# Context products of the first layer's experts: 512 columns wide, even and odd inner steps on separate groups of the array

## The reference, cut to what matters

```
def ec_moe(h, w_r, w1, w3, w2):
    cap = max(1, EC_CAPACITY * n // N_EXPERTS)            # 64 for x, 32 for context
    gate, idx = lax.top_k(jnp.swapaxes(aff, 1, 2), cap)   # each of 16 experts takes cap tokens
    xin = jax.vmap(lambda hb, ib: hb[ib])(h, idx)
    hid = silu(einsum('becd,edf->becf', xin, w1)) * einsum('becd,edf->becf', xin, w3)
    ye = einsum('becf,efd->becd', hid, w2) * gate[..., None]
    # the rows of ye are added back at their tokens' places
```

## Time and profile before

| | |
|---|---|
| median of 3 runs | 4251.18 us (4249.46 to 4256.13) |
| the profiled execution, its own time | 4257.33 us |
| its span, first to last instruction | 4255.5 us |
| mean granted TensorE clock | 0.979 of full speed |
| PE busy | 4008.4 us, 94% of the span |
| expert stage of the first layer | from 2447.6 to about 3002.5 us of the span |

### The profile page before, as it was taken

One profiled execution on the slowest core, in us unless ns is written; L12 is line 12 of the kernel. 1 busy time (PEld: TensorE's weight loads), 2 busy tenths in 40 slices (PEclk: granted clock), 3 DMA queues, 4 the chain that ended last, 5 costly groups with the idle time before them and its releaser, 6 DMA issues. The chain is left out here.

```text
span 4255.5 us, 65552 instructions
## 1 busy us (share of the span) xinstructions
PE 4008.4 (94%) x28448; PEld 2718.6 (64%) x28448; DVE 1677.8 (39%) x2603; ACT 1050.9 (25%) x2204; POOL 816.8 (19%) x640
## 2 busy tenths in 40 slices
PE   8999999999999899898999799999899999979888
PEld 6788889887888667566555443333576678833332
DVE  3685755374444442627434300000436364421102
ACT  2212522222111221616211321112315152221111
POOL 2100023113451021112233101000121234400000
PEclk9999999999999999999999899999999999989999
DMA  3584300122232212010112399999320102389997
GB/s 111 207 280 146 90 16 4 54 90 74 85 101 75 67 56 87 6 60 1 60 60 99 129 379 388 388 386 356 105 87 26 60 21 99 119 327 428 426 427 307
DMA packets 194194, 668.89 MB, mean 157 GB/s; under 512 B 11750, under 2 KB 75942, under 8 KB 169334
## 3 DMA queue, kind: packets, MB, share of 16 engines
q1 hardware_dynamic: 188022, 644.01, 40.1%
q0 software_dynamic: 5888, 20.70, 1.6%
HBM read 642.52 MB, written 22.15 MB: 156 GB/s over the span
## 5 line engine op out<-in xcount | busy, mean ns | idle before, releaser
L521 PE MATMUL psum<-arena 128*128 128x264 f32 (+2 forms) x7280 | 1829.8, 414 | 46.1 <-ACT arena L1513 19.4
L521 PEld LDWEIGHTS psum<-arena 128*128 128x128 f32 x7280 | 1386.7, 191 | 485.6 <-issue 47.9
L1397 PE MATMUL psum<-arena 128*64 128x512 f32 x3072 | 697.7, 601 | 43.7 <-DMA arena<-in_w_e 39.4
L1397 PEld LDWEIGHTS psum<-arena 128*64 128x64 f32 x3072 | 211.7, 137 | 466.8 <-issue 425.4
L553 ACT ACTIVATE arena<-psum 128x256 f32<-128x256 f32 (+2 forms) x405 | 169.3, 418 | 910.0 <-PE psum L521 878.8
L452 POOL TENSOR_TENSOR arena<-arena 128x512 f32<-128x512 f32 (+1 forms) x114 | 162.1, 1422 | 1025.6 <-PE psum L521 1025.6
L2367 DVE TENSOR_TENSOR arena<-arena,psum 128x512 f32<-128x512 f32 x32 | 22.0, 687 | 787.2 <-PE psum L1405 532.5
L382 PE MATMUL psum<-arena 128*128 128x265 f32 (+2 forms) x1120 | 257.8, 388 | 3.3 <-ACT arena L3059 3.3
L382 PEld LDWEIGHTS psum<-arena 128*128 128x128 f32 (+1 forms) x1120 | 209.8, 189 | 43.5 <-ACT arena L3059 3.7
L2813 PE MATMUL psum<-arena 64*64 64x64 f32 x7424 | 226.1, 219 | 8.7 <-issue 4.5
L2813 PEld LDWEIGHTS psum<-arena 64*64 64x64 f32 x7424 | 224.2, 135 | 11.7 <-issue 8.9
(11 more groups left out here) (417 smaller groups left out, 3916.4 us busy)
## 6 DMA issues: line engine op xcount, KB each, us to landing
arena<-in_w_e SPq DMA_DIRECT2D x192, 2048.0 KB, 12.8
arena<-in_w_in SPq DMA_DIRECT2D x38, 2048.0 KB, 8.1
arena<-in_w_ada SPq DMA_DIRECT2D x24, 2048.0 KB, 8.4
arena<-in_ffn_up SPq DMA_DIRECT2D x22, 1024.0 KB, 7.5
arena<-in_w_branch SPq DMA_DIRECT2D x6, 2048.0 KB, 8.2
arena<-in_ffn_down SPq DMA_DIRECT2D x8, 1408.0 KB, 8.1
arena<-in_w_in SPq DMA_DIRECT2D x16, 512.0 KB, 4.4
arena<-in_w_out SPq DMA_DIRECT2D x4, 2048.0 KB, 8.1
```

The costliest lines, as they stand in the source:

```text
L521: mm = pe.matmul(PS[:, bank, 0:cn], loaded, moved, start=fresh and k == 0, stop=k == h - 1, skip_group_check=not fresh)
L1397: mm = pe.matmul(PS[c * HD:c * HD + HD, b + (m > 0), :], x(kk), w[:, k, c * BW:c * BW + BW], start=(kk == 0), stop=(kk == KT - 1))
```

## The change

The context block has, per inner step, two matmuls of 512 columns in place of four of 256. Even inner steps go to the column groups 0 and 1 of the array, odd ones to the groups 2 and 3. So the partitions 0 to 63 of bank b+2 collect the sum over the even steps, with 512 columns on each of two groups of 32 partitions, and the partitions 64 to 127 the sum over the odd steps; the bank is full, and gate, up and down use it one after the other. The two sums are added at eviction: ACT copies the upper half to on-chip memory (`part_c`, semaphore c_part), DVE adds it to the lower half (`sum_c`, semaphore c_sum).

With it:

- PE waits for the sum of gate(e) before the context block of up(e), first half.
- The hidden context rows lie on 64 partitions with 512 columns. Their four transposes have 64 rows x 128 columns as stationary operand and stream 64 columns, where they had 128 rows x 64 columns and streamed 128; the copy after them (L1793 now) is one instruction instead of two.
- ACT: silu_c(e+1) stands ahead of take_ye(e), and reads on-chip memory; take_ye's context part is a copy, a wait for the sum and two pieces of 32 x 512 instead of four of 32 x 256.
- DVE: three sums per expert are added; sum_c("down", 15) stands ahead of `spread` and `add_tokens` after the last expert. `layer_scalars` moves ahead of the first sum.

```
+        HIDC, CPART = [H, H + BW], {"gate": H + 2 * BW, "up": H + 3 * BW, "down": H + 2912}
+        c_order = [("gate", 0), ("up", 0)]
+        for e in range(N_EXP):
+            c_order += [("gate", e + 1), ("down", e), ("up", e + 1)] if e + 1 < N_EXP else [("down", e)]
+        c_step = {x: i + 1 for i, x in enumerate(c_order)}
+        low, high = (0, HD), (HD, P)
...
+                    if half == 0 and m == 1:
+                        wt(pe, "c_sum", c_step["gate", e])
                     for k in range(4):
                         kk = half * 4 + k
-                        for c in range(4):
-                            mm = pe.matmul(PS[c * 32:c * 32 + 32, b + 2, (m > 0) * CTX:(m > 0) * CTX + CTX], xc(kk),
-                                           w[:, k, c * CTX:c * CTX + CTX], start=(kk == 0), stop=(kk == KT - 1))
+                        for c in range(2):
+                            r = (k % 2 * 2 + c) * 32
+                            mm = pe.matmul(PS[r:r + 32, b + 2, :], xc(kk), w[:, k, c * BW:c * BW + BW],
+                                           start=(kk < 2), stop=(kk >= KT - 2))
...
-                        tr = pe.transpose(PS[0:HD, b + 2, c * P:c * P + P], A[:, hid + BW + c:hid + BW + CTX:4], ident)
+                        hidc = HIDC[e % 2] + c
+                        tr = pe.transpose(PS[:, b + 2, c * HD:c * HD + HD], A[0:HD, hidc:hidc + BW - c:4], ident[0:HD, 0:HD])
...
+            def part_c(kind, e):
+
+                if kind == "up" and e:
+                    wt(act, "c_sum", c_step[kind, e - 1])
+                wt(act, "slab_used", slab_at[e, ("gate", "up", "down").index(kind), 1] + 1)
+                inc(nc.scalar.activation(at(CPART[kind], BW, *low), PS[HD:P, 3 * (e % 2) + 2, :], ACT.Copy), "c_part")
...
+                    part_c("gate", e)
+                    wt(act, "c_sum", c_step["gate", e])
+                    hidden = at(HIDC[e % 2], BW, *low)
+                    inc(nc.scalar.activation(hidden, hidden, ACT.Silu), "siluc")
...
-                    for c in range(4):
-                        r = slice(c * 32, c * 32 + 32)
-                        ins = nc.scalar.activation(at(yec + c * CTX, CTX, q * 32, q * 32 + 32),
-                                                   PS[r, b + 2, CTX:2 * CTX], ACT.Copy,
+                    part_c("down", e)
+                    wt(act, "c_sum", c_step["down", e])
+                    for c in range(2):
+                        ins = nc.scalar.activation(at(yec + c * BW, BW, q * 32, q * 32 + 32),
+                                                   at(CPART["down"], BW, c * 32, c * 32 + 32), ACT.Copy,
...
                 if e + 1 < N_EXP:
                     silu_x(e + 1)
+                    silu_c(e + 1)
                 take_ye(e)
-                if e + 1 < N_EXP:
-                    silu_c(e + 1)
+                if e + 1 < N_EXP and not last:
+                    part_c("up", e + 1)
...
+            def sum_c(kind, e):
+                wt(dve, "c_part", c_step[kind, e])
+                part = at(CPART[kind], BW, *low)
+                inc(V.tensor_tensor(at(HIDC[e % 2], BW, *low) if kind == "gate" else part, part,
+                                    PS[0:HD, 3 * (e % 2) + 2, :], ALU.add), "c_sum")
...
                 if not last:
+                    sum_c("up", e)
                     wt(dve, "siluc", e + 1)
-                    ins = V.tensor_tensor(at(hid + BW, CTX), at(hid + BW, CTX), PS[:, b + 2, CTX:2 * CTX], ALU.mult)
+                    wt(dve, "c_sum", c_step["up", e])
+                    hidc = at(HIDC[e % 2], BW, *low)
+                    ins = V.tensor_tensor(hidc, hidc, at(CPART["up"], BW, *low), ALU.mult)
...
+                if not last:
+                    if e + 1 < N_EXP:
+                        sum_c("gate", e + 1)
+                    sum_c("down", e)
                 if e + 1 < N_EXP:
                     hidden(e + 1)
```

More of the change, by code:

```diff
@@ L1391, in expert_slab, with half_product @@
                 return at(ES[j % n_slots], SLOT).rearrange("p (k n) -> p k n", k=4)
-            def half_product(b, w, half, x, xc, m, groups=0):
+            def half_product(b, w, half, x, xc, m, e, groups=0):
                 for k in range(4):
@@ L1417, in up @@
                 half_product(3 * (e % 2), w, half, lambda kk: at(XS[e // 2 % 2] + kk * P + e % 2 * CAP, CAP),
-                             lambda kk: at(XSC[e // 4 % 2] + kk * P + e % 4 * CAPC, CAPC), m,
+                             lambda kk: at(XSC[e // 4 % 2] + kk * P + e % 4 * CAPC, CAPC), m, e,
                              groups=e // 4 + 1 if half == 0 and m == 0 else 0)
@@ L1436, in down @@
                 half_product(3 * (e % 2), w, half, lambda kk: at(turned + kk * CAP, CAP),
-                             lambda kk: at(turned + BW + kk * CAPC, CAPC), 2)
+                             lambda kk: at(turned + BW + kk * CAPC, CAPC), 2, e)
             wt(pe, "cols", 1)
@@ L1761, in silu_x @@
                 inc(nc.scalar.activation(at(HID[e % 2], BW), PS[:, 3 * (e % 2), :], ACT.Silu), "silu")
+            def part_c(kind, e):
[3 more added lines that the diff above has]
+                inc(nc.scalar.activation(at(CPART[kind], BW, *low), PS[HD:P, 3 * (e % 2) + 2, :], ACT.Copy), "c_part")
             def silu_c(e):
                 if not last:
-                    wt(act, "slab_used", slab_at[e, 1, 1] + 1)
-                    inc(nc.scalar.activation(at(HID[e % 2] + BW, CTX), PS[:, 3 * (e % 2) + 2, 0:CTX], ACT.Silu), "siluc")
+                    part_c("gate", e)
+                    wt(act, "c_sum", c_step["gate", e])
+                    hidden = at(HIDC[e % 2], BW, *low)
+                    inc(nc.scalar.activation(hidden, hidden, ACT.Silu), "siluc")
             def take_hidden(e):
@@ L1773, in take_hidden @@
                 if not last:
[L1774 to L1777, removed]
+                    ins = nc.scalar.activation(at(turned + BW, CTX).rearrange("p (h c s) -> p c h s", h=2, s=CAPC),
+                                               PS[:, b + 2, 0:CTX].rearrange("p (c h s) -> p c h s", c=4, h=2), ACT.Copy)
                 inc(ins, "hid_taken")
@@ L1809, in _ @@
             silu_c(0)
+            if not last:
+                part_c("up", 0)
             for e in range(N_EXP):
@@ L2396, in _ @@
                 spread(PTG[0], 0, "spread_x", SEQ)
-            hidden(0)
             if not last:
                 layer_scalars(step, l + 1)
+                sum_c("gate", 0)
+            hidden(0)
             for e in range(N_EXP):
```

## The result

The changed kernel takes 4265.26 us (median of 7 runs, 4261.99 to 4269.58) against 4251.31 for the kernel before (7 runs): a ratio of 1.0032, with an interval of 1.0023 to 1.0042. It is 14 us slower.

What follows compares the result with a forecast made beforehand. PE's blocks were taken to bound the expert stage; ACT and DVE count only where PE waits. -0.9 + 5.5 + 0.8 + 3.0 + 0.4 = +8.8 us on the 4251.18 median gave 4260.0 us, range 4252 to 4266.

Steps and rivals of the forecast that it cites:

- The step that split the block into rounds: Context block, 96 times: columns set the time, excess sits at the ends; 1.855 against 1.865 us, -0.9 us in all.
- Rivals 1 and 2: Context blocks: records cost, per round (4253 us; 0.20 together with rival 3) or per record on the issue path (4230; 0.03).
- Rival 5: Context blocks: groups with different weights do not run side by side; block 3.6 us instead of 1.86, +165 us; chance 0.03.
- The transposes: Four context transposes, 16 times: mode changes and uncovered first weight loads cost 0.43 or 0.24 us more, +5.5 us.
- The sign named for it: Turns: first context transpose to L1337 or L1397 takes about 0.75 us, where 0.43 and 0.53 stood.
- rival 3: Context transposes: new ones cost no more than the old, -1.1 instead of 5.5 us, 4253.4; 0.20 together with rival 1.
- Beside PE: Expert stage: ACT's and DVE's added work, some 2 us each per expert, is covered by PE's blocks; 0.
- The last expert: Uncovered turn of expert 15: operands ready 1.0 us later, transposes add 0.2, one ACT copy saves 0.37; +0.8 us.
- Behind the last expert: DVE's chain after down(15): last sum and one-hot tables delay the first addition from 3002.95 to near 3005.95, +3.0 us.
- its own sign: Behind the last expert: DVE's first addition 3.4 us behind the last matmul of down(15) instead of 0.4.
- The clock: One-hot matmuls behind the last expert: low clock may last longer; guess half a microsecond, between 0 and 3.4; +0.4 us.
- Rival 4: Down(15) and one-hot matmuls: one more half-clock spell each, up to 1.7 us apiece; +3.4, 4263.4 us; chance 0.14.

Runs made afterwards that it cites:

- The whole-array kernel: Changed kernel with the four context transposes of a turn reading all 128 partitions and using the whole array; 4263.34 us, ratio 1.0019 to the kernel before.
- the other two kernels with the late tail: Changed kernel with context transposes on the whole array, 4263.34 us; kernel before with DVE waiting for expert 15's context result before tables and first addition, 4262.35 us.
- either repair of the change: Changed kernel with context transposes on the whole array, 4263.34 us; or with DVE's tables early and the last sum between fourth and fifth additions, 4259.86 us.
- the kernel with the tail alone: Kernel before, with DVE waiting for expert 15's context result before the one-hot tables and first addition; 4262.35 us, ratio 1.0020.

## Why the prediction was right where it was, and where it failed

**The context blocks.** Right. The step that split the block into rounds and found the excess at its ends gave 1.855 us; the block has 1.85 to 1.86. Rivals 1 and 2 (records cost) are out: half as many records leave the block as it was. Rival 5 is out too: four groups with two different sets of weights run side by side.

**The transposes.** The mechanism was right: a change of mode is paid at each border, with the first weight load behind it. The size was 5.5 for 4.7 measured: the step put 0.43 us to a turn before L1343 (measured 0.38) and 0.24 otherwise (0.18). Of the two first loads, L1343's was 0.10 us as worked out, and that of the new form 0.05 (0.62 - 4 x 0.12 - 0.09), where the prediction had 0.10: 15 x 0.05 is the 0.8. The sign named for it, about 0.75 us from the first context transpose to what follows, came out as 0.62, since besides this the 0.09 for entering the mode shows ahead of that transpose (L1434 to L1438, 0.68 for 0.59). The whole-array kernel shows the mechanism, and rival 3 falls with it.

**Beside PE.** Right: no wait of PE for c_sum shows in the turns; the block behind the new wait starts on time.

**The last expert.** 0.8 predicted, 0.9 measured, by the path named: 1.1 more of waiting, where 1.0 was predicted, and 0.2 less in the turn, as predicted.

**Behind the last expert.** Here the prediction failed in one term. It had DVE's new order right, and the sum at its time: 2.8 us from the first transpose to the tables, as worked out (3009.35 - 3006.59 = 2.76). Then it gave the tables "0.74 us", the duration that their row had at 2987.22. That row was taken while GpSimd stood idle; in the place they were moved to, GpSimd runs four instructions of 2.4 us. The term was 0.74 and measured 4.86. The trace of before held the other half already: GpSimd starts its four sums there at 3003.11, and L461, from 3005.54 to 3007.90, covers the place that the prediction gave to the tables (3005.3 to 3006.0). The prediction did not look. By its own sign DVE's first addition was to come 3.4 us behind the last matmul of down(15); it came 7.6 us behind.

**The clock.** "Half a microsecond is my guess" was low. Along the chain of eight additions the half rate costs (3019.09 - 3014.14) - (3007.14 - 3002.95) = 0.8 us, and the other two kernels with the late tail show the same (4.95 and 4.96 us for the chain). The one-hot matmuls take 0.7 us more, so 1.5 in all. The 0.7 is less firm: they take 7.59, 7.46 and 7.01 us in the three executions with the late tail, and 5.60 to 7.38 in the others. That is part of rival 4: the stretch in which PE idles, grown by 4 us more than foreseen, brought the longer spell.

Rival 4 named a second spell, over down(15), if PE idled longer at the last turn. It does, 3.24 us (2.28 and 0.96) instead of 2.47. The x block behind it is as long as before in the two executions compared (5.28 us from start to start). But it took 6.19 to 6.60 in five of the six other kernels with the changed turn, and 5.25 and 3.58 in the other two with the old one. So the change may cost a further microsecond there in most executions; that is not shown, and the 13.3 us do not hold it.

Together: 4.1 for the tables and 1.1 for the clock too low, 0.8 for the transposes too high; 8.8 + 4.4 = 13.2, against 13.3 in the stretch and 14 in the medians. That 4265.26 still lay in the range is in part luck: its upper end was made of rival 4 and of dearer transposes, and no term stood for slower tables, the largest error of the sum.

## What to carry to other kernels

Streaming products are priced by columns and by borders: count how often the array is divided anew, not how many instructions there are; here each border between an x and a context block costs 0.14 us, and putting blocks of the same kind side by side gave 0.23%, more than either repair of the change by itself. A duration moved to another place in an engine's order is only worth what it was if its neighbours on the other engines are the same there: before taking 0.74 us from a row, look at what GpSimd does at the new place. And an addition "at eviction" is not free where the eviction has no cover: at the last expert, one sum ahead of a chain, with the tables that it held back, cost more than all the other 47 sums together.

## What the runs showed of the hardware that I had not expected

- A `TENSOR_SCALAR` of 128 x 512 in on-chip memory (0.5 us alone) took 2.5 us beside GpSimd's `TENSOR_TENSOR` in the changed kernel and 2.2 in the kernel with the tail alone, and the one of 128 x 256 behind it (0.3 us alone) 2.4 in both. Each ended 0.1 to 0.3 us behind the GpSimd instruction that was under way when it started; with GpSimd held back the two were at their own duration again. `SCALAR_TENSOR_TENSOR` with its first input in PSUM, beside the same GpSimd work, stayed at 0.48.
- A transpose on 64 of 128 rows with 64 streaming columns is no cheaper than one of 128 x 128: from one to the next it is 0.12 us in either form, and the smaller one pays 0.3 us for its mode in a turn with L1343 (2.45 us for 2.13).
- The records of two 512-column blocks on column groups with different weights ran at the streaming rate, 0.43 us a round.
